# A Strassen feed-forward on one core: low parts of three weight quarters from GpSimd to VectorE, passes reordered, closing tiles cut anew

## What is computed

```
hn2 = rmsnorm(h, norm_mlp)
h = h + jnp.square(jax.nn.relu(hn2 @ w_up)) @ w_down        # D 1024, D_FF 4096
y = rmsnorm(h, norm_final)                                  # y_prompt without the 16 meta tokens, and y_sample
```

## Time and profile before

| what | us |
|---|---|
| median of 3 runs (1168.94 to 1172.07) | 1171.07 |
| the profiled execution | 1170.56 |
| its span, first to last instruction | 1168.8 |
| PE busy | 1145.3 (98%) |
| DVE busy | 764.9 (65%) |
| ACT busy | 434.7 (37%) |
| POOL busy | 551.0 (47%) |
| the down stage, its first matmul to its last | 813.5 to 1154.8 |

### The profile page before, as it was taken

How to read it: one execution, slowest core, us unless ns; L and a number is a source line. 1 busy time by engine, 2 the same in 40 slices (tenths; PEclk the granted TensorE clock), 3 DMA queues, 4 the chain that set the end, 5 groups by cost and what they waited for, 6 DMA issues and landing times.

```text
span 1168.8 us, 22531 instructions
## 1 busy us (share of the span) xinstructions
PE 1145.3 (98%) x8689; PEld 1119.8 (96%) x8689; DVE 764.9 (65%) x1141; ACT 434.7 (37%) x853; POOL 551.0 (47%) x541
## 2 busy tenths in 40 slices
PE   9999999999999999989999999999999999999996
PEld 7899999999999999989999999999898999999996
DVE  4355446456355676787777776777866677777756
ACT  6423313214124433533333333335434444444413
POOL 0154242253150431044232322323989998888992
PEclk9999999999999999999999999999999999999999
DMA  6431211211201222254435353437854553454213
GB/s 202 132 110 36 79 50 54 74 54 54 74 19 57 80 89 87 74 163 134 166 118 181 109 166 130 138 120 257 277 186 129 177 169 103 146 176 136 89 38 146
DMA packets 154007, 139.79 MB, mean 120 GB/s; under 512 B 6809, under 2 KB 118146, under 8 KB 153916
## 3 DMA queue, kind: packets, MB, share of 16 engines
q1 hardware_dynamic: 148814, 135.50, 36.3%
q10 hardware_dynamic: 5102, 3.05, 0.9%
HBM read 98.07 MB, written 40.47 MB: 119 GB/s over the span
## 4 chain that ended last, share of the span: by engine, by line
PE 46%; POOL 3%; DVE 3%; DMA 1%; issue 1%; ACT 0%; SPq 0%; ACTq 0%; POOLq 0%; DVEq 0%
PE pair L1819 15%; PE pair L1820 15%; PE pair L1821 15%; POOL dn_lo L755 2%; DMA m_raw<-m_dram 1%; DVE m_lo L1440 1%; DVE y_out L1557 1%; PE pair L1870 0%; DVE hid L1585 0%; POOL dn_s L743 0%; DVE hid L1459 0%; POOL dn_s L745 0%; ACT m_hi L1058 0%; POOL dn_s L748 0%; POOL dn_s L746 0%
## 5 line engine op out<-in xcount | busy, mean ns | idle before, releaser
L1819 PE MATMUL pair<-m_hi,dn_hi 128*128 128x258 f32 x896 | 256.5, 286 | 8.3 <-DVE a L1591 2.8
L1819 PE MATMUL pair<-b_hi,up_hi 128*128 128x258 f32 x896 | 255.0, 285 | 3.2 <-DVE hid L1497 2.2
L1820 PE MATMUL pair<-m_lo,dn_hi 128*128 128x258 f32 x896 | 254.3, 284 | 0.0
L1821 PE MATMUL pair<-m_hi,dn_lo 128*128 128x258 f32 x896 | 254.1, 284 | 0.0
L1820 PE MATMUL pair<-b_lo,up_hi 128*128 128x258 f32 x896 | 253.6, 283 | 0.0
L1821 PE MATMUL pair<-b_hi,up_lo 128*128 128x258 f32 x896 | 252.2, 282 | 0.0
L1620 PE MATMUL pair<-x_hi,w_both 128*128 128x344 f32 (+2 forms) x576 | 188.7, 328 | 0.0
L1622 PE MATMUL pair<-x_hi,w_both 128*128 128x344 f32 (+2 forms) x576 | 184.3, 320 | 0.0
L1621 PE MATMUL pair<-x_lo,w_both 128*128 128x344 f32 (+2 forms) x576 | 184.2, 320 | 0.0
L1819 PEld LDWEIGHTS pair<-m_hi,dn_hi 128*128 128x128 f32 x896 | 169.7, 189 | 11.1 <-POOL dn_lo L755 7.9
L1591 DVE TENSOR_TENSOR hid<-pair,hid 128x516 f32<-128x516 f32 (+1 forms) x194 | 124.5, 643 | 78.9 <-PE pair L1821 77.6
(11 more groups left out here) (205 smaller groups left out, 2141.4 us busy)
## 6 DMA issues: line engine op xcount, KB each, us to landing
m_raw<-m_dram SPq DMA_DIRECT2D x56, 516.0 KB, 5.0
m_dram<-hid SPq DMA_DIRECT2D x64, 258.0 KB, 2.3
up_raw<-w_up_dram SPq DMA_DIRECT2D x32, 512.0 KB, 5.0
dn_raw<-w_down_dram SPq DMA_DIRECT2D x128, 128.0 KB, 2.4
w_raw<-w_in_dram SPq DMA_DIRECT2D x28, 512.0 KB, 3.7
m_dram<-hid SPq DMA_DIRECT2D x16, 774.0 KB, 3.8
h_dram<-hid SPq DMA_DIRECT2D x8, 516.0 KB, 3.2
h_in<-h_dram SPq DMA_DIRECT2D x16, 258.0 KB, 4.3
```

The lines of the kernel that those rows point to most:

```text
L1819: m_.matmul(to, shs[k], mhs[k], start=STARTS[i] and k == 0, stop=False, skip_group_check=more)
L1820: m_.matmul(to, shs[k], mls[k], start=False, stop=False, skip_group_check=more)
L1821: ins = m_.matmul(to, sls[k], mhs[k], start=False, stop=k == last, skip_group_check=more)
```

## The change

Low parts of weights 0, 2 and 5 (RAW) of sets 5 to 31 are made by DVE (`raw_low`), and `pool_ready` counts what POOL still makes; the places are in RAW_LOW, one product after the split's. AHEAD now covers all sets. `mid_step` is replaced by MID_HIGH and MID_LOW, two tables by product number within a block. In block 0, ACT in place of DVE copies product 0 to a1. In the last and the first up units, splits and low parts move by some products. The closing tiles are cut at 0, 128, 256, 260, 388 and 516; the tile of 260 to 388 has 6 of its 8 transposes and three quarters of its squares made before the last products, and outputs inside the passes are made in two parts. PE's half passes take 260 and 256 columns in place of 258.

```diff
@@ -84,8 +84,10 @@
-FINAL_AT = {(NW, 3): 0, (NW + 1, 0): 1, (NW + 1, 5): 2, (NW + 2, 3): 3}
-NORM_AT = {(NW + 1, 1): 0, (NW + 1, 3): 1, (NW + 2, 1): 2, (NW + 2, 6): 3}
+FINAL_AT = {(NW, 3): 0, (NW, 6): 1, (NW + 1, 3): 2, (NW + 1, 6): 3, (NW + 2, 2): 4}
+NORM_AT = {(NW, 6): (0, 0), (NW + 1, 0): (0, 1), (NW + 1, 2): (1, 0), (NW + 1, 3): (1, 1), (NW + 1, 6): (2, 0), (NW + 2, 0): (2, 1),
+           (NW + 2, 2): (3, 0), (NW + 2, 3): (3, 1), (NW + 2, 5): (4, 0), (NW + 2, 6): (4, 1)}
+EARLY_AT = (NW + 2, 4)
 
@@ -104,9 +106,8 @@
-def mid_step(n):
-
-    return {0: {4: 0}, 1: {1: 1, 4: 2}, 2: {1: 3, 4: 4}, 3: {1: 5, 4: 6}}[n]
+MID_HIGH = ({11: 0, 13: 1, 15: 2, 17: 3, 20: 4, 22: 5, 24: 6}, {4: 0, 6: 1, 8: 2, 12: 3, 15: 4, 19: 5, 22: 6})
+MID_LOW = ({12: 0, 15: 1, 17: 2, 19: 3, 22: 4, 24: 5, 26: 6}, {6: 0, 9: 1, 12: 2, 16: 3, 19: 4, 23: 5, 26: 6})
 
 
@@ -131,13 +132,40 @@
 AHEAD = {}
-for _wi in range(5, 10):
+for _wi in range(5, NW):
     for _i in range(7):
-        AHEAD.setdefault(min(28 + (28 * (_wi - 5) + 4 * _i) // 5 + 1, 55), []).append((_wi, _i))
-
-
-FINAL = [(l, c, c + P) for l in range(2) for c in (0, P)] + [(0, 256, 384), (None, 496, HALF), (0, 384, 496), (1, 256, 384), (1, 384, 496)]
-REST = 5
+        AHEAD.setdefault(max(30 + 62 * (_wi - 5) // 10 + 55 * _i // 100, 7 * (_wi - 2) + _i), []).append((_wi, _i))
+
+
+RAW, SUMS = (0, 2, 5), (1, 3, 4, 6)
+RAW_FROM = 5
+RAW_LOW = {}
+for _f in AHEAD:
+    for _wi, _i in AHEAD[_f]:
+        if _i in RAW:
+            RAW_LOW.setdefault(_f + 1, []).append((_wi, _i))
+
+
+def pool_ready(wi, i):
+
+    return 7 * wi + i + 1 if wi < RAW_FROM else 7 * RAW_FROM + 4 * (wi - RAW_FROM) + SUMS.index(i) + 1
+
+
+EDGE = (0, 2 * P + 4, HALF)
+FINAL = [(l, c, c + P) for l in range(2) for c in (0, P)] + [(None, 2 * P, EDGE[1]), (0, EDGE[1], 388), (1, EDGE[1], 388), (1, 388, HALF), (0, 388, HALF)]
+REST, FIRST_LATE = 4, 5
+EARLY_F, LATE_F = (0, 1, 2, 4, 5, 6), (3, 7)
+Y_FREE = {4: 1, 5: 1, 6: 1, 7: 1, 8: 3}
+
+
+def dn_cols(ts):
+
+    return (0, HALF) if len(ts) == 2 else (EDGE[ts[0]], EDGE[ts[0] + 1])
+
+
@@ -589,7 +618,9 @@
-                    sp.wait_ge(dn_ready, 7 * wi + 7)
+                    sp.wait_ge(dn_ready, pool_ready(wi, 6))
+                    if wi >= RAW_FROM:
+                        sp.wait_ge(raw_ready, 3 * (wi - RAW_FROM) + 3)
@@ -756,13 +789,13 @@
             for wi in range(NW):
                 down_sum(wi)
-                for i in range(7):
+                for i in range(7) if wi < RAW_FROM else SUMS:
                     down_low(wi, i)
...
-                c0, c1 = TQ * ts[0], TQ * (ts[-1] + 1)
+                c0, c1 = dn_cols(ts)
@@ -772,17 +805,14 @@
...
             for q in range(NW - 4, ND):
                 close(q)
                 if q == NW:
-                    pool.wait_ge(closed, 3)
-                    gather(0)
-                if q >= NW:
-                    pool.wait_ge(dn_read, 7 * q + 7)
-                    pool.wait_ge(closed, 3 * (q - NW + 5))
-                    gather(DN[q][1])
+                    pool.wait_ge(closed, 12)
+                    for n in range(4):
+                        gather(n)
@@ -1065,11 +1095,12 @@
-                      (0, 6): (), (1, 0): ((1, 4), (1, 5)), (1, 1): ((1, 6), (2, 0)), (1, 2): ((2, 1),), (1, 3): ((2, 2),), (1, 4): ((2, 3), (2, 4))}
+                      (0, 6): ((1, 4), (1, 5), (1, 6)), (1, 0): (), (1, 1): ((2, 0),), (1, 2): (), (1, 3): (), (1, 4): ((2, 1), (2, 2)), (1, 5): ((2, 3), (2, 4)),
+                      (1, 6): ((2, 5), (2, 6))}
@@ -1092,12 +1125,12 @@
-                        if i:
-                            mid_split(i - 1)
+                        for j in ((), (0,), (1,), (2,), (3,), (4, 5), (6,))[i]:
+                            mid_split(j)
                         down_split(0, i)
@@ -1108,29 +1141,36 @@
-                    if b < BLOCKS - 1 and i in mid_step(n):
-                        mid_split(7 * (b + 1) + mid_step(n)[i])
+                    if b < BLOCKS - 1 and 7 * n + i in MID_HIGH[b > 0]:
+                        mid_split(7 * (b + 1) + MID_HIGH[b > 0][7 * n + i])
+                    if b == 0 and i == 0:
+                        act.wait_ge(dn_done, 7 * q + 1)
+                        s.activation(a1[:, n, :].rearrange("p (t c) -> p t c", c=TQ), pair[BANK[0]][:, :, 0:TQ], ACT.Copy).then_inc(a1_copied, 1)
                     if q < 4:
                         down_split(q + 1, i)
-                    elif q < 8:
+                    else:
                         for wi, j in AHEAD.get(7 * q + i, ()):
                             down_split(wi, j)
-                    elif q + 2 < NW:
-                        down_split(q + 2, i)
-                    if q == 0 and i == 3:
+                    if q == 0 and i == 5:
                         squared(LASTU, 3)
-                    if q == 0 and i == 0:
-                        mid_split(6)
...
+                fs = 0
+                if i == FIRST_LATE:
+                    fs = 3 * P
+                    act.wait_ge(fT_done, i + 1)
+                    s.activation(sq_f[:, :, 0:fs], final_bank(i)[:, :, 0:fs], ACT.Square, accum_out=ssq_p).then_inc(fsq_done, 1)
...
@@ -1477,7 +1517,8 @@
-                    (1, 0): ((1, 4), (1, 5)), (1, 1): ((1, 6), (2, 0)), (1, 2): ((2, 1),), (1, 3): ((2, 2),), (1, 4): ((2, 3), (2, 4))}
+                    (1, 0): (), (1, 1): ((1, 4), (1, 5)), (1, 2): ((1, 6), (2, 0)), (1, 3): (), (1, 4): ((2, 1), (2, 2)), (1, 5): ((2, 3), (2, 4)),
+                    (1, 6): ((2, 5), (2, 6))}
@@ -1516,13 +1557,15 @@
-                    if q == 1 and i < 3:
-                        for j in ((0, 1), (2,), (3,))[i]:
-                            mid_sum(0, j)
+                    if q == 1 and i >= 4:
+                        scaled(q, i - 3)
+                    if q == 1 and i in (1, 2):
+                        mid_sum(0, 2 * i - 2)
+                        mid_sum(0, 2 * i - 1)
@@ -1543,25 +1586,49 @@
+            def final_norm(i, part=None):
...
+                else:
+                    f0, f1 = CH * part, CH * part + CH
+                    ins = d.scalar_tensor_tensor(out=y_out[i % 4][0:rows, f0:f1], in0=final_bank(i)[0:rows, part, :], scalar=rstd_f[0:rows, j:j + 1],
+                                                 in1=gain_f[0:rows, f0:f1], op0=ALU.mult, op1=ALU.mult)
+                    if part:
+                        ins.then_inc(f_ready, 1)
...
+            def raw_low(wi, i):
+
+                n, j = dn_slot(wi), RAW.index(i)
+                dve.wait_ge(dn_high, 7 * wi + i + 1)
+                d.tensor_tensor(dn_lo[n][i][:, :, :], dn_raw[wi % 2][:, 2 * A_OP[i][0] + A_OP[i][1], :, :], dn_hi[n][i][:, :, :], ALU.subtract).then_inc(raw_ready, 1)
 
             for q, (b, n, ts) in enumerate(DN):
-                c0, c1 = TQ * ts[0], TQ * (ts[-1] + 1)
+                c0, c1 = dn_cols(ts)
@@ -1578,7 +1645,10 @@
                     if i == 0 and b == 0:
-                        d.tensor_copy(to, src).then_inc(dn_read, 1)
+                        dve.wait_ge(a1_copied, q + 1)
+                        if q:
+                            dve.wait_ge(dn_read, 7 * q)
+                        dve.sem_inc(dn_read, 1)
@@ -1589,21 +1659,23 @@
-                    if q == 0 and i < 2:
-                        mid_low(5 + i, 0)
-                        mid_low(5 + i, 1)
-                    if q == 0 and i == 2:
+                    if q == 0 and i < 4:
+                        mid_low(5 + i // 2, i % 2)
+                    if q == 0 and i == 4:
                         scaled(LASTU, 3)
                     if q == 1 and i < 4:
                         mid_sum(LASTU, i)
+                    for wi, j in RAW_LOW.get(7 * q + i, ()):
+                        raw_low(wi, j)
                     if b < BLOCKS - 1:
-                        for back in (1, 2):
-                            if i - back in mid_step(n):
-                                mid_low(7 * (b + 1) + mid_step(n)[i - back], back - 1)
+                        for half in range(2):
+                            if 7 * n + i - half in MID_LOW[b > 0]:
+                                mid_low(7 * (b + 1) + MID_LOW[b > 0][7 * n + i - half], half)
                     if (q, i) in NORM_AT:
-                        final_norm(NORM_AT[(q, i)])
-
-            for i in range(4, len(FINAL)):
+                        final_norm(*NORM_AT[(q, i)])
+
+            first_sums()
+            for i in range(FIRST_LATE, len(FINAL)):
                 final_norm(i)
@@ -1853,19 +1925,24 @@
-            def final_transposes(i):
+            def final_transposes(i, fs=range(KT), early=False):
 
                 l, c0, c1 = FINAL[i]
-                pe.wait_ge(closed, 12 if i < 4 else 21)
-                if i == 4:
+                if early:
+                    pe.wait_ge(closed, 18)
+                    pe.wait_ge(dn_read, 7 * (ND - 1))
+                else:
+                    pe.wait_ge(closed, 12 if i < FIRST_LATE else 21)
```

(26 more changed lines are left out.)

90 lines of the change are left out of this document (51 added, 39 removed).

## The result

| what | before | changed |
|---|---|---|
| median, us | 1171.57 (4 runs) | 1188.55 (4 runs, 1187.89 to 1191.27) |
| ratio | 1 | 1.0152, 95% interval 1.0127 to 1.0176 |
| the profiled execution, us | 1170.56 | 1188.57 |
| its span | 1168.8 | 1186.8 |

A forecast was written before the change was run, and what follows sets the result against it. PE was taken as the bound (busy 1145.3 of 1168.8 us), losing only short waits, mostly for DVE's sums. Terms +15.5 - 3.7 - 3.2 - 0.9 = +7.7 on 1170.56 gave 1178.3 us; range 1164.0 to 1182.5.

The forecast's parts named there:

- step 1: Passes 9 to 27, behind products 6 and 3: DVE's added low parts collide with POOL and delay PE, +15.5 us.
- step 2: Early down passes: relieving POOL ends its late sums; 7.9 of 11.6 us of waiting stay, -3.7 us.
- step 3: Start of the up stage: low parts now stand behind the reads, so both PE waits go, -3.2 us.
- step 4: Closing tiles: -2.8 us behind the last product, less added transposes and waiting ahead of it, -0.9 us in all.
- A: Behind product 6, DVE's half goes ahead of POOL's sum, costing 0.1 us per pass: 1166.9 us, chance 0.18.
- B: Behind product 6, POOL's low part of weight 6 slips out and nothing collides: 1154.9 us, chance 0.15.
- C: Later passes: the price is paid in only half, about 7.5 in place of 15.5: 1170.3 us, chance 0.17.
- D: Early passes: nothing is saved there, 1182.0 us, chance 0.08.

The follow-up runs named there:

- experiment 3: The changed kernel without the work of POOL's four sums per weight set from set 10 on, so its down product is incomplete: 1173.96 us in one run.
- experiment 4: The changed kernel with DVE's two operations of a turn swapped, half of an activation first and the weight's low part behind it: 1187.96 us in one run.
- Experiment 2: The kernel before with only the three low parts of sets 5 to 31 moved to DVE, each one product after its split: 1190.27 us, ratio 1.0157.
- experiment 1: The changed kernel with the three low parts back on POOL, all else of the change kept: 1163.97 us, ratio 0.9937.
- experiment 9: The changed kernel with all low parts on POOL and the splits of sets 5 and on at the places of the kernel before: 1167.48 us, one run.
- experiment 10: The changed kernel with all low parts on POOL and the splits and halves of activations at the places of the kernel before: 1169.39 us, one run.
- experiment 12: Changed kernel, low parts on POOL, next block's first activation split sooner from block 3 on, first three up units as before the change: 1162.96 us, ratio 0.9932.
- experiment 7: The changed kernel with DVE's low parts of both quarters 2 and 5 one product later: 1171.92 us (10 runs), ratio 1.0008.

## Why the prediction was wrong

The direction and the mechanism of the steady passes were right. The size was not (+7.7 forecast, +17.0 measured), and the mechanism of the early passes was wrong. The profiled span grew by 18.0, 10.3 more than forecast: 4.1 of it in step 1, 2.0 in step 2, 2.0 in step 3 and 2.2 in step 4. By its own steps:

- **Step 1, the turns of products 6 and 3: right in kind, too small by 4.1.** 0.7 us forecast, 0.73 measured, by the locks in the order foreseen (experiments 3 and 4). The 0.2 in the turn of product 3 is there as well (product 5 to product 6 takes 1.65 us in pass 13 of the changed kernel, 1.43 before). The sum of 15.5 was too small by three terms. Behind each wait PE takes 0.07 us more for the product (1.52 for 1.45); the 0.2 falls in 13 passes and not in 11; and the wait of a turn of product 6 lands in the pass behind it, so that 20 passes pay, 9 to 28, and not 19. 20 x 0.80 + 13 x 0.27 = 19.5, and 19.6 was measured. (Pass 25 loses only 0.17 ahead of product 2, and pass 9 loses 0.65 more ahead of product 3; these nearly cancel.)
- **Step 2, the early waits: the step that failed.** It took the earlier trace rows for a chain that begins with POOL's load and that nothing else of the change would break, and valued the relief of POOL at 3.7 us. Experiment 2 bears out the reading for the old order: there the relief ends the 4.5 us of pass 8. But the new order ends them by itself, with POOL just as full (experiment 1), so that in the change the relief has nothing to give there. The rest of the change gains 8.8 us early, where the forecast gave the new order 1.4 (4.3 less the 2.9 kept) and took 1.4 back for a POOL still catching up. Of the 8.8, the old places of the splits bring back 2.4 and those of the activations 2.8 (experiments 9 and 10: 96.56 and 96.92 us for passes 0 to 8, against 94.16); what the others hang on is not shown. And 7.1 of the 8.8 are lost again (94.16 to 101.23 us) by a wait that the forecast did not ask for: the low part's own, for ACT's split, with the reads queued behind it. In pass 5 alone the profiled execution lost 5.7 us. The step counted what the new operations take and not what they wait for. That it missed by only 2.0 in all (-1.7 for -3.7) is luck: two large terms that it did not have nearly cancel.
- **Step 3, the start of the up stage: the gain did not come.** -3.2 forecast, -1.2 in the one profiled execution, nothing by experiment 12. Kernels with the change's code there and a full clock behind it start pass 0 at 812.3 to 813.4, against 813.45 before. The two waits did not go; one of 3.0 us stands behind 532.6 in their place, behind DVE's low parts of 1.78 us each beside POOL's sums.
- **Step 4, the closing tiles: half right.** Behind the last product starts, 1.5 us are saved (in the kernel before the last output was ready 10.2 us behind the last product; now it is 8.1, where 7.5 was forecast). Ahead of it, the half passes cost 1.7 us more than before even without DVE's low parts (experiment 1: 36.82 against 35.12), near the 1.9 forecast; the low parts add 1.1. (At the earlier trace rows's 1.06 per 8, the 14 transposes counted as 1.5 are 1.9; the forecast's sum was 0.4 too low there.) With POOL making the low parts the closing is +0.3 in all, where -0.9 was forecast.
- **The rivals.** A needed DVE's half ahead of POOL's sum, and that came in one turn; B needed no collision, and 20 passes show one. C had the price in half of the passes; all 20 pay. D ("nothing is saved early", 1182.0) was nearest, but the changed kernel saved 1.7 us early. What lies between D and the measured time, and so above the range, is 4.1 in the steady passes, 2.0 ahead of pass 0 and 2.2 in the closing, less the 1.7.

What stays open: pass 5 took 15.87 us in the changed kernel, and 12.50 and 12.59 in experiments 3 and 4, whose operations there are the same (in 4 in another order). The traces show where the 3.3 us are. ACT's split, which waits for its load, starts 1.9 us behind the start of pass 5 in the changed kernel, and 0.2 and 0.1 us ahead of it in the other two, and product 2 starts 2.0 us later. Products 2 and 3 then take 4.30 us in place of 2.96, beside a granted clock of 0.68 (last section) where the others have 1.00. Why the load came late in that execution, and how much of the early loss returns in every one, is not shown.

The Trainium skill's page "SBUF — State Buffer", section "Who interferes with whom", says that DVE instructions with two SBUF inputs contend with GpSimd's reads, and that the order of issue decides who blocks. The turns above agree: a low part of 0.41 us alone takes 0.90 behind POOL's, and at the end of pass 24, where DVE's half was first, POOL's sum took 1.06 for 0.74. The Trainium skill's page "Perfetto Trace Analysis", section "Optimizing Scalar/DVE Operations", says that moving work between the two engines might not help. The runs agree that it did not; how much it cost depended on the turn, 24.6 us against POOL in one place and 8 in the other (experiments 1 and 7).

## What to carry to other kernels

In this kernel the operations that moved to a less busy engine took their waits along. So look at what such an operation waits for and at what stands behind it in the new queue, before counting its duration. A busy share says nothing of that: in the stretches shown, POOL at 98% cost nothing (experiment 1), and DVE at 94% cost nothing (experiment 7), while DVE at 87% with two locks in one short turn cost a tenth of every pass (the change). And split a change into its parts before judging it: here one part lost 24.6 us and hid a gain of 0.6% in the rest.
